# High and low parts of 28 weight tiles made by DMAs instead of by ScalarE and VectorE

## The reference

```
h    = rms_norm(x, norm_mix_pre);  proj = h @ w_in          # u, v, q, k, v_att, gates
x    = x + rms_norm(merged @ w_o, norm_mix_post)            # gated spatial unit and window attention, merged
hf   = rms_norm(x, norm_ff_pre)
ff   = square(relu(hf @ w_ff_in)) @ w_ff_out                # w_ff_in 1024x4096, w_ff_out 4096x1024
out  = x + rms_norm(ff, norm_ff_post)
```

## Time and profile before

| | |
|---|---|
| runs | 785.15, 785.18, 785.74 us |
| profiled execution | 785.12 us, its span 783.4 us |
| instructions | 9921 |
| busy | PE 765.7 us, PEld 640.7, DVE 529.3, ACT 365.2, POOL 58.4 |
| DMA | 80.29 MB, mean 102 GB/s over the span |
| mean granted clock of TensorE | 0.996 of 2.4 GHz |

### The profile page before, as it was taken

One profiled execution on the slowest core, in us unless ns is written; L12 is line 12 of the kernel. 1 busy time (PEld: TensorE's weight loads), 2 busy tenths in 40 slices (PEclk: granted clock), 3 DMA queues, 4 the chain that ended last, 5 costly groups with the idle time before them and its releaser, 6 DMA issues.

```text
span 783.4 us, 9921 instructions
## 1 busy us (share of the span) xinstructions
PE 765.7 (98%) x3640; PEld 640.7 (82%) x3640; DVE 529.3 (68%) x883; ACT 365.2 (47%) x609; POOL 58.4 (7%) x110
## 2 busy tenths in 40 slices
PE   7999999999999999999999999999999999999994
PEld 6888888888887888888888998888887888878873
DVE  5624667677777336885635779746895579667897
ACT  4522656666565744232325545544443444334542
POOL 3000000022223003000001200000000000000002
PEclk9999999999999999999999999999999999999998
DMA  8333232212132532326331452136003620262002
GB/s 295 109 114 101 70 92 79 83 55 82 55 83 80 188 101 61 114 75 242 107 108 54 161 186 57 54 139 211 27 3 104 259 65 1 56 240 81 0 1 108
DMA packets 91581, 80.29 MB, mean 102 GB/s; under 512 B 2833, under 2 KB 77585, under 8 KB 91537
## 3 DMA queue, kind: packets, MB, share of 16 engines
q1 hardware_dynamic: 90864, 79.70, 31.5%
q10 hardware_dynamic: 672, 0.01, 0.0%
HBM read 77.60 MB, written 2.10 MB: 102 GB/s over the span
## 4 chain that ended last, share of the span: by engine, by line
PE 90%; DVE 6%; ACT 1%; DMA 1%; issue 0%; SPq 0%; POOL 0%; DVEq 0%; POOLq 0%; ACTq 0%
PE acc L1382 26%; PE acc L1384 26%; PE acc L1383 26%; DVE w_lo L1213 2%; PE aux L1383 1%; PE aux L1384 1%; PE aux L1382 1%; DVE sum L1236 1%; DMA w_raw<-in_w_in 1%; PE aux L1569 1%; PE aux L1495 1%; PE aux L1494 1%; PE aux L1504 1%; PE acc L1523 1%; PE acc L1520 1%; PE aux L1477 1%
## 5 line engine op out<-in xcount | busy, mean ns | idle before, releaser
L1382 PE MATMUL acc<-actB_hi,w_hi 128*128 128x512 f32 (+1 forms) x544 | 207.3, 381 | 0.8 <-DVE sum L1318 0.8
L1384 PE MATMUL acc<-actB_hi,w_lo 128*128 128x512 f32 (+1 forms) x544 | 205.4, 378 | 0.0
L1383 PE MATMUL acc<-actB_lo,w_hi 128*128 128x512 f32 (+1 forms) x544 | 205.2, 377 | 0.0
L931 DVE TENSOR_TENSOR w_lo<-w_raw,w_hi 128x1024 fp32r<-128x1024 f32 x72 | 87.8, 1223 | 83.9 <-ACT w_hi L648 83.1
L1382 PEld LDWEIGHTS acc<-actB_hi,w_hi 128*128 128x128 f32 x544 | 102.5, 188 | 19.6 <-DVE w_lo L1209 1.6
L1384 PEld LDWEIGHTS acc<-actB_hi,w_lo 128*128 128x128 f32 x544 | 102.4, 188 | 18.9
L1383 PEld LDWEIGHTS acc<-actB_lo,w_hi 128*128 128x128 f32 x544 | 102.5, 188 | 18.1
L648 ACT ACTIVATE w_hi<-w_raw 128x1024 fp32r<-128x1024 f32 x72 | 75.4, 1052 | 71.1 <-PE acc L1384 68.8
L1382 PE MATMUL acc<-w_hi,actB_hi 128*128 128x512 f32 x160 | 62.7, 392 | 1.5 <-DVE actB_lo L941 1.3
L1384 PE MATMUL acc<-w_hi,op_lo 128*128 128x512 f32 x160 | 63.5, 397 | 0.0
L1383 PE MATMUL acc<-w_lo,op_hi 128*128 128x512 f32 x160 | 63.4, 396 | 0.0
(11 more groups left out here) (192 smaller groups left out, 1292.1 us busy)
## 6 DMA issues: line engine op xcount, KB each, us to landing
w_raw<-in_w_in SPq DMA_DIRECT2D x44, 512.0 KB, 3.9
w_raw<-in_w_ff_in SPq DMA_DIRECT2D x32, 512.0 KB, 4.0
down_raw<-in_w_ff_out SPq DMA_DIRECT2D x16, 1024.0 KB, 6.9
w_raw<-in_w_b SPq DMA_DIRECT2D x8, 512.0 KB, 3.6
w_raw<-in_w_a SPq DMA_DIRECT2D x8, 512.0 KB, 3.5
w_raw<-in_w_o SPq DMA_DIRECT2D x8, 512.0 KB, 3.8
x<-in_x SPq DMA_DIRECT2D x4, 512.0 KB, 7.5
x<-in_x SPq DMA_DIRECT2D x1, 2048.0 KB, 9.0
```

The costliest lines, as they stand in the source:

```text
L931: nc.vector.tensor_tensor(w_lo[:, j], w_raw[:, j], w_hi[:, j].bitcast(F32), ALU.subtract).then_inc(lo_made, 1)
L1382: nc.tensor.matmul(o, a_hi, b_hi, start=first, stop=False)
L1383: nc.tensor.matmul(o, a_hi, b_lo, start=False, stop=False)
L1384: return nc.tensor.matmul(o, a_lo, b_hi, start=False, stop=last)
```

## The change

For the 28 up tiles after the first four, no raw tile is loaded. GpSimd's queue issues two DMAs for each: one from `w_ff_in` straight into `w_hi`, whose type float32r makes it convert (`load_hi`), when TensorE is done with the unit four before; and one from `w_ff_in` again into `w_lo` with `accum_op` add (`add_lo`), after ScalarE has written the negated high part there (`negate_up`, in the place of `hi_up`). So low = -high + value. TensorE waits for this second DMA (`up_lo`) instead of `lo_made`. VectorE has nothing to do for an up tile. `hi_made` and `lo_made` now count only the first tiles and the product items (`halves_made`).

In GpSimd's queue the order per chunk is hi(0), hi(1), lo(0), hi(2), lo(1), and so on. SP's queue keeps the first four up tiles and then has only w_ff_out: in chunks 1 to 3 those loads wait for all low parts of the chunk before, and besides for up unit 0 (loads 0 and 1) or 1 (loads 2 and 3) of their own chunk to be done. The descriptor scratch grows to 4096 bytes.

```diff
-SCRATCH = 1024
+SCRATCH = 4096
...
+def halves_made(r):
+    c, n = divmod(r, ITEMS)
+    return U_FF + SLOTS + c * 2 * len(PRODUCTS) + max(n - FF_UNITS + 1, 0)
+def slot_use(m):
+    r = ff_unit(m)
+    return 16 * sum(ff_unit(x) % SLOTS == r % SLOTS for x in range(SLOTS, m + 1))
...
             def load_down(c, j):
                 if c:
-                    sp.wait_ge(lo_made, U_FF + item(c, 0))
+                    sp.wait_ge(lo_made, halves_made(item(c, 0) - 1))
+                    sp.wait_ge(pe_done, UNIT_DONE[U_FF + item(c, j // 2)])
...
+            for m in range(SLOTS):
+                slot_free(U_FF + m)
+                load_columns(m, w_ff_in_v, slice(m * P, (m + 1) * P))
+            sp.wait_ge(a_lo, GROUPS)
             for c in range(CHUNKS):
-                for n in range(6):
-                    load_up(c * FF_UNITS + n)
...
+                for j in range(PAIRS):
+                    load_down(c, j)
...
+            def load_hi(m):
+                r = ff_unit(m)
+                pool.wait_ge(pe_done, UNIT_DONE[U_FF + r - SLOTS])
+                nc.gpsimd.dma_start(stationary(w_hi, r % SLOTS), up_columns(m)).then_inc(up_hi[r % SLOTS], 16)
+            def add_lo(m):
+                r = ff_unit(m)
+                pool.wait_ge(neg_made, m - SLOTS + 1)
+                nc.gpsimd.dma_start(stationary(w_lo, r % SLOTS), up_columns(m),
+                                    accum_op=ALU.add).then_inc(up_lo[r % SLOTS], 16)
+            for c in range(CHUNKS):
+                tiles = range(SLOTS if c == 0 else c * FF_UNITS, (c + 1) * FF_UNITS)
+                load_hi(tiles[0])
+                for m in tiles:
+                    if m + 1 in tiles:
+                        load_hi(m + 1)
+                    add_lo(m)
...
-            def hi_up(m):
-                j = up_slot(m)
-                act.wait_ge(w_loaded[j], 16 * up_loads(m))
-                r = ff_unit(m)
-                act.wait_ge(pe_done, UNIT_DONE[U_FF + r - SLOTS])
-                nc.scalar.activation(w_hi[:, r % SLOTS], w_raw[:, j], ACT.Copy).then_inc(hi_made, 1)
+            def negate_up(m):
+                j = ff_unit(m) % SLOTS
+                act.wait_ge(up_hi[j], slot_use(m))
+                nc.scalar.activation(w_lo[:, j], w_hi[:, j].bitcast(F32), ACT.Copy, scale=-1.0).then_inc(neg_made, 1)
...
                 if n < FF_UNITS:
-                    m = c * FF_UNITS + n
-                    nc.vector.tensor_tensor(w_lo[:, r % SLOTS], w_raw[:, up_slot(m)],
-                                            w_hi[:, r % SLOTS].bitcast(F32), ALU.subtract).then_inc(lo_made, 1)
+                    return
...
-                    pe.wait_ge(lo_made, U_FF + item(c, n) + 1)
+                    pe.wait_ge(up_lo[item(c, n) % SLOTS], slot_use(c * FF_UNITS + n))
```

More of the change, by code:

```diff
@@ L404, in hybrid_block @@
         x1_made = sem("x1_made")
+        up_hi = [sem(f"up_hi{j}") for j in range(SLOTS)]
+        up_lo = [sem(f"up_lo{j}") for j in range(SLOTS)]
+        neg_made = sem("neg_made")
         down_loaded = [sem(f"down_loaded{j}") for j in range(PAIRS)]
@@ L628, in _, with up_columns @@
                     inv_sqrt(ssq[:, 3, t:t + 1], 3, t, rstd_x1)
+            def up_columns(m):
+                return w_ff_in_v[:, 0:KT, m * P:(m + 1) * P]
+            def load_hi(m):
[14 more added lines that the diff above has]
+                    add_lo(m)
             for first, n in ((2, 0), (0, 4)):
@@ L865, in hi_ahead @@
                 if n < FF_UNITS:
-                    hi_up(c * FF_UNITS + n)
+                    negate_up(c * FF_UNITS + n)
                 else:
@@ L1205, in lo_ahead @@
                     return
-                dve.wait_ge(hi_made, U_FF + r + 1)
                 if n < FF_UNITS:
-                    m = c * FF_UNITS + n
-                    nc.vector.tensor_tensor(w_lo[:, r % SLOTS], w_raw[:, up_slot(m)],
-                                            w_hi[:, r % SLOTS].bitcast(F32), ALU.subtract).then_inc(lo_made, 1)
[L1211 to L1214, removed]
+                    return
+                dve.wait_ge(hi_made, halves_made(r))
+                k, h = divmod(n - FF_UNITS, 2)
+                nc.vector.tensor_tensor(moving(w_lo, r % SLOTS), right_raw(PRODUCTS[k], h),
+                                        moving(w_hi, r % SLOTS).bitcast(F32), ALU.subtract).then_inc(lo_made, 1)
             def weight_sum(c, name):
@@ L1643, in operands @@
             def operands(c, name, h):
-                pe.wait_ge(lo_made, U_FF + product_item(c, name, h) + 1)
+                pe.wait_ge(lo_made, halves_made(product_item(c, name, h)))
                 pe.wait_ge(op_lo_made, 3 * (c * PAIRS + 2 * h + 1) + {"P1": 1, "P4": 2, "P2": 2}.get(name, 3))
```

## The result

The changed kernel takes 869.96 us (median of 4 runs, 868.78 to 870.04); the ratio to the kernel before is 1.107, 95% interval 1.106 to 1.109. That is 84.8 us more. The profiled execution took 869.95 us, its span is 868.0 us against 783.4.

The account below looks back on a forecast made before the run. TensorE's nearly unbroken matmuls were taken as the bound. Late up tiles cost 13.9 us in each of three chunks and 7.7 in chunk 0, less two waits: 785.1 + 49.4 - 0.8 = 834 us, range 788 to 935 us.

Parts of the forecast that it names:

- Direction and bound: Feed-forward part: TensorE bounds, VectorE's and ScalarE's work is hidden, giving up early loads makes it slower; chance of slower 0.88.
- First tile ready 12.0 us after its slot: Each chunk's first up tile: high part 4.0, negation 1.06, low part 6.9 us in series; due at 8.3 us.
- The sign named for this term: Landing medians of the converting and adding DMAs near 4.0 and 6.9 us would confirm the terms.
- Pace 6.9 us: Later up tiles come 6.9 us apart, the landing time of a 1024 KB load, against TensorE's 5.44 us.
- Rival 2: Writing descriptors holds GpSimd's queue about as long as the transfers: pace 10.9 us, 145 us lost, 930 us; chance 0.21.
- Free while they don't double: SP's later w_ff_out loads: wanted 10.9 us on, landing in 6.9, 9.1 at worst, so no cost.
- That delay falls on the start of chunk 1 ... so I add nothing: Chunk 0: ScalarE's copies of P2's banks wait behind tile 2's negation; the pace sets chunk 1's end anyway; nothing added.
- TensorE's clock: Up stages: a fall of TensorE's granted clock would mean a loss not counted; no size given.
- The sum again: Last up tile late by 13.9 us in each of three full chunks and 7.7 us in chunk 0, together 49.4 us.
- Rival 1: Transfers keep TensorE's pace; only each chunk's first tile is late, 0.8 to 3.7 us, four times: 788 to 800 us; chance 0.25.
- Rival 3: VectorE's work locks out GpSimd's descriptor writing: 19 us a tile, 340 us lost, 1125 us; chance 0.05.
- Rival 4: Not slower: two landings of 3.6 us each fit before the first tile is due; 784.4 us; chance 0.12.

Follow-up runs that it names:

- the kernel with both edits: Changed kernel with descriptor scratch 8192 bytes instead of 4096 and chunks 1 to 3's w_ff_out loads cut to 8 KB each: 819.73 us, ratio 1.044.

## Why the prediction was right, and what it sized wrong

**Direction and bound: right.** TensorE was the path, VectorE's 34.3 us and ScalarE's copies lay beside it, and with the head start given up the transfers' own times fell on it. The size was too small: a loss of 48.6 us was forecast, 84.8 us were measured.

**First tile ready 12.0 us after its slot.** In chunk 2 the slot is free at 633.56 and the first matmul starts at 646.30: 12.7 us. By parts, 4.5 for the high part (4.0 taken), 1.06 for the negation, 6.6 for the low part (6.9 taken), the rest between them. It is 13.3 us in chunk 0 (455.7 to 469.03) and 14.4 in chunk 3 (740.7 to 755.12). The sign named for this term fails in half: the landing medians are 6.6 and 6.6, not 4.0 and 6.9, for only a high part with nothing beside it lands in 4.5.

**Pace 6.9 us.** The number was right, the reason not. I had taken it from the row of a transfer of twice the bytes, and named the transfer engines, close to full, as support. The rows give 6.9 to 7.0 us, but the pace is that of one add after another in a scratch that has no room for two; the prediction nowhere asks what the scratch holds. That both come to 6.9 is luck. With 8192 bytes and no collision the up units are 5.44 us apart again, so the transfer engines can do it. Rival 2 (GpSimd's queue as the bound) had the right place and the wrong mechanism; writing holds the queue for 0.89 and 1.57 us, 2.5 us a tile, not 10.9.

**"Free while they don't double": the step that was mis-sized.** I held the loads of w_ff_out against their own landing, which indeed stayed near the old one (7.9 us median). Beside the others I had spread their 4 MB over eight units, 1.6 us each. They come in one burst at some 300 GB/s: an add lands after 16.0 us and a high part after 17.2, 6.6 otherwise. Priced at 0, measured at 26.2 us by the kernel without them.

**"That delay falls on the start of chunk 1 ... so I add nothing".** The delay is there, 8.2 us once, where chunk 2's start waits 4.8. But the last tile of chunk 1 is as late as that of chunk 2 (24.1 and 24.2 us, below), so adding nothing was right as far as the trace shows; no run tried it by itself. In the kernel with both edits, where the pace is 5.44 us, it stays: 9.0 us of wait, against 4.8 to 5.9 at the other starts.

**TensorE's clock.** Named as a loss not counted. TensorE's busy time is 21.9 us longer, at a mean granted clock of 0.963 against 0.996. With a full clock a part of it would turn into longer waits for the next tile, so it is not all the clock's price; how much, no run shows.

**The sum again, with measured ends.** The last tile of a chunk was to start 60.3 us after the first slot is free (32.7 in chunk 0). Measured: 34.1 in chunk 0 (455.7 to 489.8), 70.5 in chunk 1, 70.6 in chunk 2, 72.3 in chunk 3, against 25.0 and 46.4 us due: 9.1 + 24.1 + 24.2 + 25.9 = 83.3 us of the 84.6. Chunk 0, where no load of w_ff_out comes in between, was forecast to 1.4 us; the other three are 10 to 12 us over. The collision, 8.7 us a chunk by the kernel without it, is most of that.

**The rivals.** Rival 1 (the pace kept, only starts late, 788 to 800 us) is what is left when room and collision are taken away, but at 820, since the starts wait longer than 3.7 us (4.8 to 9.0) and cost clock. Rival 3, VectorE locking the writing out, did not occur: the issues of the last adds of chunks 1 to 3 (590.15, 697.43 and 806.38 us), during which VectorE worked with tensor_tensor, took 1.58 to 1.59 us, and those with VectorE idle 1.55 to 1.59. Of the high parts' issues (least 0.889 us, median 0.894) the one long one, 1.59 us at 749.37, stands behind an add with VectorE all but idle. The Trainium skill says that tensor_tensor was not seen to stall a DMA from GpSimd's queue (SBUF — State Buffer, "Who interferes with whom"), and the trace agrees; its two-port case has no row here. Rival 4 needed two landings of 3.6 us; they were 4.5 at the least and 6.6.

By the Trainium skill (DMA: Bandwidth & Descriptors, "Anatomy of one DMA") a DMA from GpSimd takes 2.0 us plus its bytes at 436 GB/s, an estimate of 3.2 us for a tile. That is low here: the trace has 4.5 us at the least for the converting DMA and 6.5 for the adding one, in pieces of 512 bytes.

## What to carry to other kernels

Removing an operation that already hid beside the bound engine was worth nothing here (VectorE's 34.3 us); what counts is whether its replacement can start as early, and here every transfer became one that starts when the ring slot is free. Hold such a chain against the time until the tile is due, and hold every transfer that shares the engines against it too, not only against its own use. And in an in-order queue a wait for a landing stops everything written behind it: put what frees another engine first.

## What the hardware showed that I had not expected

- An adding DMA takes more of GpSimd's descriptor scratch than a converting one of the same bytes (two converting second DMAs went out 2.8 us apart, adding ones 6.9 to 7.0), and the queue stands still until there is room, without a releaser in the profile. The kernel with 3072, 4096 and 8192 bytes takes 973.8, 870.0 and 847.2 us.
- 4 MB from SP's queue stretched landings on GpSimd's queue from a median of 6.6 us to 16.0 and 17.2.
- After 8.17 us of idle time TensorE ran at the lower clock level for 5.7 us (542.57 to 548.25; granted clock 0.50); its first up unit then took 8.3 us instead of 5.44, 2.9 us on top of the wait. After waits of about 1.2 us (690.26, 697.16 us) its starts stayed 0.23 us apart.
